# Forget-gate attention scores: one 128-row product in place of two, in padded buffers for each head

## The reference

```
c = cumsum(log_sigmoid(f_logit), axis=1)                 # one number per token and head
for blk in range(4):                                     # query blocks of 128 tokens
    qs, qe = blk * 128, (blk + 1) * 128
    sc = einsum('bqhd,bkhd->bhqk', q[:, qs:qe], k[:, :qe]) * scale
    sc = sc + (c[:, :, qs:qe, None] - c[:, :, None, :qe])
    sc = where(causal, sc, -inf)
    o  = softmax(sc) @ v[:, :qe]
```

## Time and profile before

| | us |
|---|---|
| median of 3 runs | 3204.73 |
| lowest and highest | 3204.52, 3204.86 |
| the profiled execution | 3206.67 |
| its span in the profile | 3204.9 |
| TensorE busy | 3127.0 (98%) |
| VectorE busy | 1766.1 (55%) |
| ScalarE busy | 1127.2 (35%) |

### The profile page before, as it was taken

How to read it: one execution, slowest core, us unless ns; L and a number is a source line. 1 busy time by engine, 2 the same in 40 slices (tenths; PEclk the granted TensorE clock), 3 DMA queues, 4 the chain that set the end, 5 groups by cost and what they waited for, 6 DMA issues and landing times.

```text
span 3204.9 us, 42789 instructions
## 1 busy us (share of the span) xinstructions
PE 3127.0 (98%) x17840; PEld 2480.5 (77%) x17840; DVE 1766.1 (55%) x2404; ACT 1127.2 (35%) x1600; POOL 62.9 (2%) x65
## 2 busy tenths in 40 slices
PE   7999999999999999999999999999999999999997
PEld 5777856788888888766788888788887767888886
DVE  4466664534354344778764344743446777643446
ACT  4432353423232223335443223432233354432233
POOL 0013300000000000000000000000000000000000
PEclk9999999999999999999999999999999999999998
DMA  6110035333332322311232332333232212333232
GB/s 253 40 33 23 30 139 184 106 99 99 95 96 94 101 96 89 98 60 53 89 102 93 99 99 88 123 98 98 93 92 92 75 48 86 99 97 98 95 92 86
DMA packets 83425, 298.49 MB, mean 93 GB/s; under 512 B 9633, under 2 KB 11297, under 8 KB 81313
## 3 DMA queue, kind: packets, MB, share of 16 engines
q1 hardware_dynamic: 83232, 295.75, 28.5%
HBM read 289.42 MB, written 6.29 MB: 92 GB/s over the span
## 4 chain that ended last, share of the span: by engine, by line
PE 92%; DVE 4%; issue 2%; ACT 2%; DMA 0%; SPq 0%; DVEq 0%; ACTq 0%
PE PS L1870 79%; PE PS L1952 3%; PE PS L2203 1%; PE PS L2186 1%; PE PS L1885 1%; PE PS L2205 1%; PE PS L2081 1%; PE PS L2224 1%; PE PS L2213 1%; ACT SPL L2259 1%; PE PS L2145 1%; PE PS L2157 0%; PE PS L2176 0%; PE PS L1905 0%; PE PS L1912 0%
## 5 line engine op out<-in xcount | busy, mean ns | idle before, releaser
L1870 PE MATMUL PS<-HS,SPL 128*128 128x512 f32 (+1 forms) x7752 | 1804.7, 393 | 7.6 <-DVE HS L2606 3.2
L1870 PEld LDWEIGHTS PS<-HS,SPL 128*128 128x128 f32 (+1 forms) x7752 | 1449.2, 188 | 330.9 <-issue 19.7
L2558 DVE TENSOR_TENSOR SPL<-RAW,SPL 128x1024 fp32r<-128x1024 f32 (+1 forms) x483 | 578.6, 1201 | 728.8 <-ACT SPL L2259 724.9
L2259 ACT ACTIVATE SPL<-RAW 128x1024 fp32r<-128x1024 f32 (+1 forms) x483 | 498.2, 1035 | 848.6 <-PE PS L1870 848.1
L1870 PE MATMUL PS<-FF,SPL 128*128 128x512 f32 x2880 | 654.6, 389 | 0.0
L1870 PEld LDWEIGHTS PS<-FF,SPL 128*128 128x128 f32 x2880 | 540.6, 188 | 112.2
L2955 DVE SCALAR_TENSOR_TENSOR CA<-AP__150,CW,CA 128x512 f32<-128x512 f32 x240 | 180.0, 750 | 6.2
L2457 ACT ACTIVATE FF<-TMP 128x512 fp32r<-128x512 f32 x88 | 55.7, 633 | 235.9 <-DVE TMP L2925 235.9
L2451 ACT ACTIVATE SA<-SA 128x512 f32<-128x512 f32 x88 | 55.5, 633 | 191.7 <-DVE SA L2915 191.7
L2915 DVE TENSOR_TENSOR SA<-PS,R 128x512 f32<-128x512 f32 x88 | 60.5, 691 | 98.8 <-PE PS L1870 98.5
L2927 DVE TENSOR_TENSOR FF<-TMP,FF 128x512 fp32r<-128x512 f32 x88 | 60.9, 692 | 66.6 <-ACT FF L2457 66.6
(11 more groups left out here) (295 smaller groups left out, 2227.2 us busy)
## 6 DMA issues: line engine op xcount, KB each, us to landing
RAW<-in_w_ff_in SPq DMA_DIRECT2D x176, 512.0 KB, 3.7
RAW<-in_w_in SPq DMA_DIRECT2D x88, 512.0 KB, 3.7
RAW<-in_w_ff_out SPq DMA_DIRECT2D x80, 512.0 KB, 3.6
RAW<-in_w_ff SPq DMA_DIRECT2D x64, 512.0 KB, 3.7
MW<-in_w_mod SPq DMA_DIRECT2D x32, 512.0 KB, 4.1
RAW<-in_w_out SPq DMA_DIRECT2D x24, 512.0 KB, 4.4
MW<-in_w_mod SPq DMA_DIRECT2D x8, 1024.0 KB, 19.5
RAW<-in_w_ple_gate SPq DMA_DIRECT2D x16, 512.0 KB, 4.1
```

Of the source, the lines that this page charges most:

```text
L1870: m = pe.matmul(o, w[x][:, r.kp + k, rows], r.T[:, r.k0 + k, y, 0:r.cols], start=r.start and k == 0 and (x, y) == (0, 0), stop=r.stop and ...
L2259: a.activation(SPL[:, s, 0, 0:n], RAW[:, s, 0:n], AF.Copy).then_inc(w_hi, 1)
L2558: v.tensor_tensor(SPL[:, s, 1, 0:n], RAW[:, s, 0:n], SPL[:, s, 0, 0:n], ALU.subtract).then_inc(w_lo, 1)
```

## The change

The rank terms move onto the same 128 rows as the product of q and k. For either parity of the head there are two buffers in f32, QZ and KZ, of 128 partitions. Of the 128 rows, 64 hold the head's q (or k), 32 the rank terms, and 32 are zero:

- ScalarE copies the head's 64 rows of q and k from QK into QZ and KZ, in a new part of `f_row`. It waits for q and k, and for the last score product of the head two before.
- VectorE writes the rank rows: of KZ in `f_row`, for each head, of QZ once per layer at the end of `f_logit`, for both parities (two instructions where CL was one).
- GpSimd sets the zero rows once per layer, in `conv_pad` (four fills).
- `f_scores` makes one f32 product of QZ and KZ, and the mask. The product of CL and RH is left out. Its waits are now those for the rank row, the copies and the zeros.
- So that the rank rows can stand on any group of 32 partitions, the forget logits are computed on all 128: the weight has 128 columns (the 8 logits 16 times over), and CF, FH and the table SEL2 have 128 partitions.

```diff
-        dense(W["w_f_2"][l], 8, HS, None, ev_f, 32)
+        dense(W["w_f_2"][l], 8, HS, None, ev_f, 128)
 ...
         def f_row(h):
             t = Rec()
             t.h, t.L, t.after, t.done = h, L, rh_after[h % 2], count(s_rh)
+            t.waits, t.copied = [qk_ready["q", h // 2], qk_ready["k", h // 2]], [count(s_qz), count(s_qz)]
             emit("f_row", t)
-            rh_ready[h] = t.done
+            rh_ready[h] = [t.done, t.copied[1], L.zeroed[h % 2][1]]
 ...
-            s.use, s.waits = use, [qk_ready["q", s.h // 2], qk_ready["k", s.h // 2], rh_ready[s.h]] if s.qb == 0 else []
+            s.use, s.waits = use, rh_ready[s.h] if s.qb == 0 else []
 ...  TensorE, f_scores
-            pe.matmul(PS[:, b, 0:n], QK[r, s.h // 2, 0, 128 * s.qb:128 * s.qb + 128], QK[r, s.h // 2, 1, 0:n],
+            pe.matmul(PS[:, b, 0:n], QZ[s.h % 2][:, 128 * s.qb:128 * s.qb + 128], KZ[s.h % 2][:, 0:n],
                       start=True, stop=False)
-            pe.matmul(PS[:, b, 0:n], CL[:, 128 * s.qb:128 * s.qb + 128], RH[:, s.h % 2, 0:n], start=False, stop=False)
 ...  ScalarE
+        def f_row(r):
+            rows = own_rows[r.h % 2]
+            for w in r.waits:
+                a.wait_ge(*w)
+            if r.after:
+                a.wait_ge(*r.after)
+            for y, Z in enumerate((QZ, KZ)):
+                a.activation(Z[r.h % 2][rows, :], QK[rows, r.h // 2, y, :], AF.Copy).then_inc(s_qz, 1)
 ...  VectorE, end of f_logit
-            v.tensor_scalar(CL[:, :], CF[:, :], SEL2[:, 0:1], SEL2[:, 1:2], ALU.mult, ALU.add).then_inc(s_cl, 1)
+            for x, rows in enumerate(rank_rows):
+                v.tensor_scalar(QZ[x][rows, :], CF[rows, :], SEL2[rows, 0:1], SEL2[rows, 1:2], ALU.mult,
+                                ALU.add).then_inc(s_cl, 1)
 ...  GpSimd, conv_pad
+            for x, set_ in enumerate(L.zeroed):
+                g.memset(QZ[x][zero_rows[x], :], 0.0).then_inc(s_zero, 1)
+                g.wait_ge(*set_[0])
+                g.memset(KZ[x][zero_rows[x], :], 0.0).then_inc(s_zero, 1)
+                g.wait_ge(*set_[1])
```

More of the change, by code:

```diff
@@ L171, in build @@
     PT2 = sb("PT2", [128, 2, 4, 512], F32, 173)
-    CF = sb("CF", [32, 512], F32, 189)
-    FH = sb("FH", [32, 512], F32R, 126)
+    CF = sb("CF", [128, 512], F32, 189)
+    FH = sb("FH", [128, 512], F32R, 126)
     CW = sb("CW", [128, 132], F32, 191)
-    SEL2 = sb("SEL2", [32, 20], F32, 191.625)
-    CL = sb("CL", [32, 512], F32R, 112)
-    RH = sb("RH", [32, 2, 512], F32R, 114)
+    SEL2 = sb("SEL2", [128, 20], F32, 191.625)
+    QZ = [sb(f"QZ{i}", [128, 512], F32, 112 + 2 * i) for i in range(2)]
+    KZ = [sb(f"KZ{i}", [128, 512], F32, 116 + 2 * i) for i in range(2)]
+    own_rows, rank_rows, zero_rows = ([slice(0, 64), slice(64, 128)], [slice(64, 96), slice(0, 32)],
+                                      [slice(96, 128), slice(32, 64)])
     RCV = sb("RCV", [128, 512], F32, 144)
@@ L225, in build @@
     s_fl, s_fa, s_fs, s_fh = sem("f_logit"), sem("f_act"), sem("f_sum"), sem("f_high")
-    s_cl, s_rh = sem("f_column"), sem("f_row")
+    s_cl, s_rh, s_qz = sem("f_column"), sem("f_row"), sem("head_padded")
+    s_zero = sem("zero_rows")
     s_cn, s_cs, s_cphi, s_cplo = sem("conv_scaled"), sem("conv_silu"), sem("conv_hi"), sem("conv_lo")
@@ L1507, in build @@
         L.l, L.last, L.cw, L.s2, L.rms, L.pad = l, last, m_cw, m_s2, m_r, count(s_apad)
+        L.zeroed = [[count(s_zero), count(s_zero)] for _ in range(2)]
         emit("conv_pad", L)
@@ L1556, in ev_f @@
             give(u)
-            q.logit, q.act, q.sum, q.high, q.done = count(s_fl), count(s_fa), count(s_fs), count(s_fh), count(s_cl)
+            q.logit, q.act, q.sum, q.high = count(s_fl), count(s_fa), count(s_fs), count(s_fh)
+            count(s_cl)
+            q.done = count(s_cl)
             slot_end[q.slot] = q.done
             L.cl = q.done
-        dense(W["w_f_2"][l], 8, HS, None, ev_f, 32)
+        dense(W["w_f_2"][l], 8, HS, None, ev_f, 128)
         qk_ready, v_ready = {}, []
@@ L2198, in f_scores @@
             b, n = s.use.b, 128 * (s.qb + 1)
-            r = slice(64 * (s.h % 2), 64 * (s.h % 2) + 64)
             for w in s.waits:
@@ L2464, in f_logit @@
         def f_logit(r):
-            t = TMP[0:32, r.slot, :]
+            t = TMP[:, r.slot, :]
             if r.after:
@@ L2538, in _ @@
                 "dft_cols": dft_cols, "f_split": f_split, "residual": residual, "relu": relu, "glu_a": glu_a, "glu_b": glu_b,
-                "conv_b": conv_b, "f_logit": f_logit, "v_turned": v_turned, "f_turn": f_turn, "f_values": f_values,
+                "conv_b": conv_b, "f_logit": f_logit, "f_row": f_row, "v_turned": v_turned, "f_turn": f_turn, "f_values": f_values,
                 "conv_out": conv_out, "gate": gate, "merge": merge, "embed": embed, "ple_gate": ple_gate,
@@ L2962, in f_logit @@
         def f_logit(r):
-            t = TMP[0:32, r.slot, :]
+            t = TMP[:, r.slot, :]
             v.wait_ge(*r.L.last)
             v.wait_ge(*r.use.mark)
-            v.tensor_tensor(CF[:, :], PS[0:32, r.use.b, :], R[0:32, :], ALU.mult).then_inc(free[r.use.b], 1)
+            v.tensor_tensor(CF[:, :], PS[:, r.use.b, :], R[:, :], ALU.mult).then_inc(free[r.use.b], 1)
             v.wait_ge(*r.use.rel)
-            v.tensor_scalar(CF[:, :], CF[:, :], vec(f"bf_{r.L.l}")[0:32, :], None, ALU.add).then_inc(s_fl, 1)
+            v.tensor_scalar(CF[:, :], CF[:, :], vec(f"bf_{r.L.l}"), None, ALU.add).then_inc(s_fl, 1)
             v.wait_ge(*r.act)
@@ L2973, in f_logit @@
             v.wait_ge(v_own, own.n)
-            v.tensor_tensor_scan(CF[:, :], ones[0:32, 0:1].to_broadcast([32, 512]), t, 0.0, ALU.mult,
+            v.tensor_tensor_scan(CF[:, :], ones[:, 0:1].to_broadcast([128, 512]), t, 0.0, ALU.mult,
                                  ALU.add).then_inc(s_fs, 1)
@@ L3004, in f_row @@
                 v.wait_ge(*r.after)
-            v.tensor_scalar(RH[:, r.h % 2, :], CF[:, :], SEL2[:, 2 + r.h:3 + r.h], SEL2[:, 10 + r.h:11 + r.h],
+            rows = rank_rows[r.h % 2]
+            v.tensor_scalar(KZ[r.h % 2][rows, :], CF[rows, :], SEL2[rows, 2 + r.h:3 + r.h], SEL2[rows, 10 + r.h:11 + r.h],
                             ALU.mult, ALU.add).then_inc(s_rh, 1)
@@ L3131, in conv_pad @@
             g.memset(AP_[:, :, 0:30], 0.0).then_inc(s_apad, 1)
+            g.wait_ge(*L.pad)
+            for x, set_ in enumerate(L.zeroed):
[3 more added lines that the diff above has]
+                g.wait_ge(*set_[1])
         does = {"c_column": c_zero, "zeros": zeros, "inv_l": inv_l, "inv_a": inv_a,
@@ L3195, in constants @@
     sel[:, 19] = 1 - 2 * low
-    c["c_sel"] = sel
+    c["c_sel"] = np.tile(sel, (4, 1))
     return {k: np.ascontiguousarray(v) for k, v in c.items()}
@@ L3234 @@
     A["w_in_2"] = np.stack([pieces(np.concatenate([wi[l][:, :1536], wi[l][:, 1544:]], 1)) for l in range(2)])
-    A["w_f_2"] = np.stack([rows(np.concatenate([wi[l][:, 1536:1544]] * 4, 1)) for l in range(2)])
+    A["w_f_2"] = np.stack([rows(np.concatenate([wi[l][:, 1536:1544]] * 16, 1)) for l in range(2)])
     A["p"] = np.stack([rows(x["p_2"][l, 0].T) for l in range(2)])
```

## The result

| | before | after |
|---|---|---|
| median of 4 runs, us | 3204.62 | 3182.04 |
| lowest and highest | 3203.96, 3204.86 | 3181.43, 3186.04 |
| the profiled execution | 3206.67 | 3181.43 |
| its span | 3204.9 | 3179.7 |
| granted clock, mean | 0.991 | 0.991 |

The changed kernel is faster: ratio 0.9929, 95% interval 0.9917 to 0.9941. The medians lie 22.6 us apart, the two profiled spans 25.2. The forecast was a gain of 36.8 us and a time of 3168 (3160 to 3178): the right sign, but a gain too large by more than half.

The account below looks back on a forecast made before the run. TensorE, busy 98% of the span, was taken as the bound. Per layer 21.2 us less work minus 2.8 of new waits, times two, gave 36.8 us off the 3204.73 median: 3168 us, range 3160 to 3178.

Parts of the forecast that it names:

- The new product: Mixer attention scores on TensorE: four widths need 2.15 us instead of 4.31, over 16 sets 34.6 us less.
- The rival of exposed loads: 128-row weight loads on TensorE are exposed: 128 instructions × 0.11, 14 us less gained, about 3182; chance 4%.
- The entry: Start of a score unit after 128-row transposes: 0.11 instead of 0.20 us, 64 times, 5.8 us less.
- The exit: End of a score unit: mask's weights load beside the 128-row product; 0.03 us each, 2 us less, bounds 0 to 3.
- The forget logits: Forget gate's projection widened to 128 columns, 60 us ahead of the first score: cost 0, without cover about 1 us a layer.
- The copies: ScalarE's 32 copies of q and k: cost on TensorE 0, bound 17.6 us if nothing covers them.
- the rival that was slower by ScalarE's queue: Copies and weight splits delay the exponential 3.3 us at 16 heads: 53 us lost against 42 gained, about 3216; chance 3%.
- What is late next: New TensorE waits in the attention for late results of VectorE and ScalarE: 2.8 us of gain lost a layer.
- bank reuse and unit 24 to 26: Scores wait for exponentials to free their two banks: 1.1 us around unit 9's bank, 1.1 at 1480, per layer.
- the wait for the pair's result: TensorE's 2.3 us wait for VectorE after the first pair of heads becomes 2.9: 0.6 us of gain lost.
- The rival of VectorE as bound: VectorE, 89% busy in the attention, lags until the statistics: another 3 to 6 us a layer lost, about 3177; chance 12%.
- The clock: Half clock after TensorE's waits may be prolonged, appear elsewhere or vanish: ±4 us around any case.

Follow-up runs that it names:

- before_f128: The kernel before with only the forget logits' path widened from 32 to 128 rows, scores keeping their three products: 3205.69 us, ratio 0.9995.
- few_copies: The changed kernel with ScalarE copying q and k only for the first two heads of a layer, later heads reusing them: 3183.8 us, ratio 0.9929.
- late_stats: The changed kernel with the convolution's statistics taken after 7 instead of 2 weight pieces and its output one dense product later: 3184.17 us, ratio 0.9928.
- two moves: Gate's sigmoids behind the attention, statistics after seven weight pieces: changed kernel 3172.69 us, kernel before 3205.91; changed kernel with five pieces 3166.47.
- after_again: The changed kernel itself, unaltered, run once more beside the later versions: 3181.97 us, ratio 0.9919 against the kernel before.

## Why the prediction was wrong

- **The new product, 34.6 us less: right.** It measured 34.1 (16 × 2.13): 0.44, 0.65 and 0.86 us stand in the rows of after. The prediction says that the 4.31 us of before contain three changes of the number of rows; they contain two, and the first (128 to 64) lies in the entry, where it is counted. The rival of exposed loads gave 3182 by its sum, which is the time measured, and it is nevertheless refuted: 128 instructions at 0.11 more would show as 1.08 for 512 keys where 0.86 stands. A time that agrees with a rival's is no proof of it. The Trainium skill, in TensorE: Matmul & The Clock Gate, Part 3 (The mechanism), lets a load overlap only where its row group differs; this case's trace does not agree (0.43 us per product of 512 columns, one after another on all rows). On 64 rows the distance is 0.53, so there something of 0.10 us stays exposed; what it is, no run shows.
- **The entry, 5.8 less: right**, 0.11 instead of 0.20. The Trainium skill, in TensorEngine Tiling (Array Packing), Key Properties, says that a change of the tiling mode drains TensorE; the trace has 0.09 us at either change of the number of rows, but also 0.10 between the two instructions on the same 64 rows, where nothing changes. So it does not show that the change is what costs; it shows that the 64-row form does.
- **The exit, 2 less: mis-sized**, mask to next product went from 0.039 to 0.028, 64 times 0.011 or 0.7 us. The lower bound was nearly the true one. A cost that stands in front of the mask is already counted in the 34.6.
- **The forget logits, 0: right** (before_f128). **The copies, 0: right** (few_copies), and with them falls the rival that was slower by ScalarE's queue: the copies cost nothing, though ScalarE's queue is part of the chain that does.
- **What is late next, 2.8 a layer: this step failed.** It was 7.3. By its own items: bank reuse and unit 24 to 26, forecast 2.2, measured 1.9 as waits of the product for PB; the wait for the pair's result, forecast 0.6 more, measured 0.5 more. These were sized well. Two places were missing, beside 0.4 for the result of a later pair (AS). One is the value product's and the turn's wait for the copy PT (3.9 + 0.8 against 0.8): the prediction laid VectorE's maximum and the exponential beside TensorE's way, but not the other thing that ScalarE's queue delivers, which stands right behind the exponential. A late maximum delays both. The other is the statistics: VectorE was expected to be as much earlier as TensorE, and it was not quite. TensorE reached them 13.9 us earlier than before, VectorE's last sums began 13.4 us earlier (1541.22 to 1527.87), so the wait was 2.7 for 2.1, and 5.8 when TensorE came 3.6 us earlier still.
- **The rival of VectorE as bound, 12%, 3177:** this came nearest to what decided, and its price was 3 to 6 us a layer in the forecast and 4.5 in the waits (7.3 less 2.8). That the sizes agree is in part luck: the rival put the loss at the statistics, where only 0.6 of it lies, while 3.9 lie at PT. Its chance was too low, because a busy share of 89% was taken as room. The argument against it was that VectorE's idle time lies where it waits for scores and shrinks by itself. This happened, from 19.3 us to 4.3 in 1384 to 1530 us. What did not shrink is VectorE's waiting for ScalarE, 12.0 us before and 13.7 after. The first lines of VectorE's waits, after:

```profile
DVE SPL L2572 <- ACT SPL L2264: 5.9, 4, 2.4
DVE SM L2883 <- PE PS L2211: 4.3, 4, 2.1
DVE AS L3027 <- ACT AS L2508: 4.2, 3, 2.2
```

- **The clock** stayed out of the account: 58.0 us at half in the span before, 57.2 after. In one version it was worth some 6 us (late_stats, 69.5 us at half).
- **The account.** 36.8 were forecast, 25.2 lie between the spans: 1.8 less saved, 9.0 more waited (14.6 less 5.6), 0.8 not assigned. The other 2.6 us between forecast and median are those between spans (25.2) and medians (22.6): the profiled run of before lay 2.0 above its median, that of after 0.6 below. To subtract from a median what was worked out on a slower profile carries such an offset.

## What to carry to other kernels

When one engine is made faster, list everything that it receives from in-order queues in the next stretch, not just the result that one has in mind: a copy that stands behind a late exponential is as late as that. Follow the hand-overs between the two helping engines, and compare arrival times: of a helper's idle time only what it spends waiting for the engine that gets faster is room, not what it spends waiting for its partner. After the change look for work that can be moved out of the helpers' common chain: here two moves that were worth nothing before it (with seven pieces) brought 9.3 us after it, 15.5 with five pieces, and each of them alone nothing in the median.

## What was not expected of the hardware

- Products on all 128 rows have no gap for their loads, while the 64-row pair cost 0.09 us at its entry, 0.10 between its two instructions and 0.09 behind it. So zero rows that are multiplied along were cheaper than a small product of its own: 0.44 us for 256 keys, where the three-product form took 0.94.
- The granted clock does not follow from the waits alone. The same kernel in two profiles (after and after_again) has one and three stretches at half clock in the first mixer, and behind the same wait of 1.7 us for MS it fell to half in one version and not in the other. Here are both, 1599 to 1606 us, the version with the late statistics:

```profile
1599.00:1606.00 7.00, 6.64 (x17) 5.25 (x18) 4.49 (x7) 2.71 (x4) 0.00 (x0) 0.55 0.45 146
```

and the one with both moves:

```profile
1599.00:1606.00 7.00, 7.00 (x32) 5.81 (x31) 5.17 (x8) 3.45 (x5) 0.00 (x0) 1.00 0.48 152
```

The wait ended at 1599.4 in the first and at 1596.8 in the second. At half clock the engine executed 17 instructions in this stretch, at full clock 32: that is the consequence, and what decides it stays open.
